# A hybrid decoder layer on one core: reordered dense stage with a 22nd weight slot, and both ends rearranged

## The chip, the core and the metric

The kernel runs on one core of a Trainium2 chip. The metric is the device time of one execution in microseconds, as the median of three runs. TensorE multiplies matrices, VectorE (DVE) and ScalarE (ACT) work on rows of data, GpSimd (POOL) does so too, and SyncE (SP) here issues every transfer from memory. All compute is float32; a "rounded" tile is one in the faster, coarser form that TensorE takes.

## What is computed

One decoder layer over 256 tokens of width 1024, cut to what matters here:

```python
mod = silu(c) @ w_ada + b_ada                       # six vectors: shift, scale, gate, twice
h = rmsnorm(x, norm1) * (1 + sc1) + sh1
proj = h @ w_in                                     # q, k, v | mLSTM q/k, v, o, i/f | gates g_a, g_m
y_a = diff_attention(q, k, v, lam)                  # 4 heads, each the difference of two softmaxes
y_m = rmsnorm(sigmoid(o) * mlstm(silu(conv(qk)), v, i, f))
merged = sigmoid(g_a) * (y_a @ w_br_a) + sigmoid(g_m) * (y_m @ w_br_m)
x = x + gt1 * (merged @ w_out)
h2 = rmsnorm(x, norm2) * (1 + sc2) + sh2
y = sum over 32 experts of gate[e] * ((silu(h2 @ w_e1[e]) * (h2 @ w_e3[e])) @ w_e2[e])   # top 2 of 8 in the top group
out = rmsnorm(x + gt2 * y, norm_f)
```

## The kernel before, in words

All weights pass once from memory, in units of 128 x 2048 floats (1 MB). A **first stage** (to 54 us) multiplies the eight row blocks of q, k and v while VectorE forms the shift and scale that the normalized input needs; each product is done in three passes, rounded weight by rounded input, rounded weight by the input's rest, weight's rest by rounded input.

The **dense stage** (54 to 242 us) works off 24 dense units: `ml0` to `ml3` (mLSTM q and k), `mv`, `mo`, `ga0` to `ga3`, `gm0` to `gm3`, the branch projections (`bra`, `brm`) and the output projection (`wo0` to `wo3`). For each, ACT writes a rounded copy (`split(d)`, line 538, into one of three slots `his`, so it must wait for the job three before), GpSimd subtracts it to leave the rest (line 515, four pieces), and TensorE multiplies (`proj` and `proj_T`, line 1379). Between them stand the attention (`scores` and `sums` on DVE, `exps` and `scale` on ACT, `mix` on DVE, `transpose_a`, `copy_a`, `times_v`) and the mLSTM (gate rows `gate_inputs`, `gate_sums`, `decay`, `numerator`, `hidden`). The 16 conditioning units ("ada") are not multiplied on TensorE: VectorE reduces each against the conditioning vector (`sums_of(i, u)`, line 913, two instructions of 128 x 1024). Dense and ada units come through the same ring of ten slots, in the order of `unit_list`; a slot is loaded again once its last unit was multiplied or summed. SP issues all loads in one fixed order, so a load whose slot is not free holds up all behind it.

The **expert stage** takes the 32 experts in eight quads. A quad needs 12 units (four each of w1, w3 and w2). They land in 21 slots (`XSLOTS`, the ring, the `his` slots and buffers that the dense stage no longer needs); `RELEASES` says which job frees each slot for its first unit, `EARLY` which of these loads are issued among the dense ones. From then on a slot is loaded again when its unit is `used`. A quad gathers its tokens (`gather`), multiplies (`up`, line 1715), transposes the hidden rows (`turn`), multiplies again (`down`, line 1726, in two halves c), VectorE scales each half by the gate (line 1287), and the result is scattered back into four banks that hold the residual sum (`scatter`, line 1670, one part for each c and token tile), while the next quad runs. If a list of tokens is over 32, further passes follow in a branch (`flag`); with these inputs none does.

At the **end** the last scattering waits for `act_end` and `dve_end`, ACT squares the four parts, VectorE makes the norm's factor, and writes each part times factor and gain (line 1335); four stores follow.

Each engine's order is the order of the code; nothing is scheduled. The unit order, the first waits and the place of the sums:

```python
for n, count in enumerate((0, 1, 1, 1, 1, 1, 1, 1, 1, 2, 0, 1, 0, 1, 1, 1, 2, 0, 0, 0)):
    units += [dense[n]] + ada(*sums[:count])
...
for h in range(HEADS):          # VectorE
    conv(h)
    scores(h)
    sums_of(3, h)
```

## Time and profile before

| | us |
|---|---|
| median of three runs | 461.53 (461.12 to 462.02) |
| the profiled execution, its own time | 461.61 |
| its span | 459.8 |
| TensorE busy | 384.4 (84%) |
| VectorE, ScalarE, GpSimd busy | 196.9, 176.5, 154.7 |
| moved from memory | 161.62 MB, 354 GB/s over the span |

A page of the profile lists busy times, then the span in 40 slices, the chain of work that ended last followed back from the end, and the costliest groups of instructions. TensorE has two clocks here, granted by the chip: 1.00 is 2.4 GHz, 0.50 is 1.2 GHz. In a timeline the bracket behind an instruction is the time that its engine had been idle, and what ended it. Busy time alone says little in this kernel, since the stages have different limits; the stretches and timelines show which engine or transfer is waited for in each.

### The profile page before, as it was taken

What the parts mean: (1) busy time and instruction counts of PE and PEld (TensorE: products, weight loads), DVE (VectorE), ACT (ScalarE), POOL (GpSimd) and SP (SyncE); (2) the same over time, 40 slices, a digit from 0 to 9 for tenths busy, and PEclk for the clock granted to TensorE, in tenths of its full rate; (3) what the DMA queues carried; (4) which work ended last, traced back from release to release, by engine and by line L of the source; (5) the groups of instructions that cost most, each with busy time, mean ns of one, the idle gap of its engine ahead of it and who ended that gap; (6) DMA issues with size and microseconds to landing.
All of it is one profiled execution on the core that took longest, in us unless ns stands there. A gap on an engine that the chain in (4) does not pass through costs nothing.

```text
span 459.8 us, 8048 instructions
## 1 busy us (share of the span) xinstructions
PE 384.4 (84%) x3326; PEld 300.4 (65%) x3326; DVE 196.9 (43%) x405; ACT 176.5 (38%) x328; POOL 154.7 (34%) x125
## 2 busy tenths in 40 slices
PE   6699999987799999989989579889897393684963
PEld 5599999887699999989967436445463261351411
DVE  3997369999731538892252130312112003001023
ACT  3677655752937856444253312141212020020012
POOL 0798766658298477869100000000000000000000
PEclk9799999997889999999999989999999799598879
DMA  8999999858849732999996999999999999999932
GB/s 335 423 419 423 419 420 420 295 203 353 324 161 424 240 141 65 386 421 419 406 374 211 427 375 422 424 420 420 420 420 422 422 419 422 420 422 420 422 128 94
DMA packets 23223, 163.23 MB, mean 355 GB/s; under 512 B 2576, under 2 KB 2704, under 8 KB 4368
## 3 DMA queue, kind: packets, MB, share of 16 engines
q1 hardware_dynamic: 23184, 162.68, 87.3%
q8 instruction: 28, 0.46, 0.4%
q14 instruction: 11, 0.09, 0.1%
HBM read 161.62 MB, written 1.05 MB: 354 GB/s over the span
## 4 chain that ended last, share of the span: by engine, by line
PE 58%; DVE 17%; DMA 13%; ACT 5%; issue 3%; SPq 2%; DVEq 0%; ACTq 0%
PE bank L1379 16%; DMA ring<-in_e 12%; PE bank L1715 10%; PE cs_b L1726 6%; PE bank L1681 5%; PE bank L1422 5%; PE bank L1670 4%; DVE ring L913 4%; PE bank L1427 3%; DVE mqk L986 3%; SPq L443 2%; PE cs_b L1379 1%; PE bank L1414 1%; DVE o_att L958 1%; PE cs_b L1408 1%
## 5 line engine op out<-in xcount | busy, mean ns | idle before, releaser
L515 POOL TENSOR_TENSOR ring_r<-ring,his_r 128x512 fp32r<-128x512 f32 x120 | 154.4, 1320 | 54.2 <-ACT his_r L538 54.1
L788 ACT ACTIVATE raw<-bank,sm 128x128 f32<-128x128 f32 x60 | 22.6, 456 | 127.4 <-PE bank L1681 127.4
L1715 PE MATMUL bank<-ring,raw 128*32 128x256 f32 x512 | 55.3, 403 | 9.0 <-DMA ring<-in_e 9.0
L538 ACT ACTIVATE his_r<-ring 128x2048 fp32r<-128x2048 f32 (+1 forms) x32 | 57.6, 1800 | 8.2 <-PE bank L1379 8.2
L1275 DVE TENSOR_TENSOR tmp<-bank,tmp 128x256 f32<-128x256 f32 x8 | 3.4, 425 | 128.0 <-ACT tmp L797 128.0
L1379 PE MATMUL bank<-his_r 128*128 128x256 f32 x304 | 45.2, 293 | 1.9 <-ACT his_r L728 1.2
L1715 PEld LDWEIGHTS bank<-ring,raw 128*32 128x32 f32 x512 | 28.4, 116 | 23.9 <-issue 15.3
L1379 PEld LDWEIGHTS bank<-his_r 128*128 128x128 f32 x304 | 40.4, 197 | 3.7 <-issue 1.4
L913 DVE CUSTOM_DVE_ANT_0 ring<-ring,cs_b 128x1024 f32<-128x1024 f32 x32 | 37.7, 1215 | 0.2
L1681 PEld LDWEIGHTS bank<-const,gm 128*128 128x128 f32 x240 | 28.4, 191 | 9.3 <-issue 7.3
L1681 PE MATMUL bank<-const,gm 128*128 128x128 f32 x240 | 30.1, 278 | 3.4 <-DVE const L1266 1.8
L1670 PE MATMUL bank<-v,const 128*128 128x512 f32 x64 | 29.0, 595 | 1.9 <-DVE sm L1320 1.9
L1715 PE MATMUL bank<-his,raw 128*32 128x256 f32 x176 | 23.3, 390 | 7.9 <-DMA home<-in_e 7.9
L1726 PE MATMUL cs_b<-ring,WT 128*32 128x512 f32 x120 | 26.1, 667 | 2.4 <-DVE WT L1280 1.6
L1379 PE MATMUL bank<-his_r,ring_r 128*128 128x256 f32 x192 | 26.9, 283 | 0.0
L1379 PE MATMUL bank<-hT_r,his_r 128*128 128x256 f32 x192 | 26.6, 280 | 0.0
L1715 PE MATMUL bank<-home,raw 128*32 128x256 f32 x112 | 21.3, 431 | 6.1 <-DMA ring<-in_e 6.1
L1379 PEld LDWEIGHTS bank<-his_r,ring_r 128*128 128x128 f32 x192 | 24.7, 192 | 0.0
L1379 PEld LDWEIGHTS bank<-hT_r,his_r 128*128 128x128 f32 x192 | 24.4, 189 | 0.0
L1287 DVE TENSOR_TENSOR v<-cs_b,o_att 128x512 f32<-128x512 f32 x16 | 11.1, 692 | 28.7 <-PE cs_b L1726 28.7
L1670 PEld LDWEIGHTS bank<-v,const 128*128 128x128 f32 x64 | 11.5, 190 | 15.5 <-issue 15.5
L1379 PE MATMUL bank<-ring_r,his_r 128*128 128x256 f32 x112 | 17.2, 300 | 4.7 <-POOL ring_r L515 4.7
(330 smaller groups left out, 726.2 us busy)
## 6 DMA issues: line engine op xcount, KB each, us to landing
ring<-in_e SPq DMA_DIRECT2D x47, 1024.0 KB, 24.7
ring<-in_rest SPq DMA_DIRECT2D x40, 1024.0 KB, 8.0
his<-in_e SPq DMA_DIRECT2D x16, 1024.0 KB, 22.5
home<-in_e SPq DMA_DIRECT2D x10, 1024.0 KB, 20.5
ring<-in_block SPq DMA_DIRECT2D x8, 768.0 KB, 20.0
o_att<-in_e SPq DMA_DIRECT2D x5, 1024.0 KB, 20.0
mqk<-in_e SPq DMA_DIRECT2D x5, 1024.0 KB, 22.8
qkT<-in_e SPq DMA_DIRECT2D x5, 1024.0 KB, 26.3
```

The lines of the kernel that those rows point to most:

```text
L515: pool.tensor_tensor(ring_r[:, slot_of(n), sl], ring[:, slot_of(n), sl], hi(d)[:, sl].bitcast(F32), ALU.subtract).then_inc(s["w_lo"], 1)
L538: act.activation(hi(d)[:, 0:WIDTH[d]], ring[:, slot_of(n), 0:WIDTH[d]], ACT.Copy).then_inc(s["w_hi"], 1)
L788: ins = act.activation(xg[:, b, k, :], source[:, j * P:(j + 1) * P], ACT.Identity, bias=S("B2", KD)[:, k:k + 1], scale=S("A2", KD)[:, k:k ...
L913: ins = dve.tensor_tensor_reduce(w, w, cs_b[:], 1.0, 0.0, ALU.mult, ALU.add, m2[:, at:at + 1])
L986: ins = dve.scalar_tensor_tensor(out=mqk[:, k, back:T], in0=seq[:, 0:T - back], scalar=col("conv_w", 8 * j + k), in1=mqk[:, k, back:T], op ...
L1379: ins = pe.matmul(out, left(k), right(k), start=(i == 0 and k == 0), stop=(i == 2 and k == nk - 1))
L1422: ins = pe.matmul(pb(f"qk{i // 2}")[:, (i % 2) * T:(i % 2 + 1) * T], w[:, i * P:(i + 1) * P], h, start=start and i % 2 == 0, stop=stop, sk ...
L1427: ins = pe.matmul(pb(f"v{tt}")[:], h[:, tt * P:(tt + 1) * P], w[:, 1024:FIRST], start=start, stop=stop, skip_group_check=True)
L1670: ins = pe.matmul(y_banks[2 * tt + c][:], ptg[:, b, tt, :], outs2[:, 512 * c:512 * c + 512], start=False, stop=stop, skip_group_check=True)
L1681: ins = pe.matmul(target[:, j * P:(j + 1) * P], xn[:, tt, k * P:(k + 1) * P], pone[:, tt].rearrange("p a n -> p (a n)"), start=(tt == 0), ...
L1715: ins = pe.matmul(up_bank[e * CAP:(e + 1) * CAP, half], xg[:, b, k, e * CAP:(e + 1) * CAP], wt[e][:, k, :], start=(k == 0), stop=(k == KD ...
L1726: ins = pe.matmul(out_banks[c][e * CAP:(e + 1) * CAP, :], hidT[:, f, e * CAP:(e + 1) * CAP], wt[e // 2][:, 2 * (e % 2) + f, :], start=(f = ...
```

## The change

In `unit_list` the ada units move behind the fifth dense unit and stand closer together later. On VectorE no sum stands among the four heads: all softmax sums, the gate rows and the mixes come first, then the eight sums of sc2's and sh2's columns in two groups, then the others, all ahead of the attention output's low halves (`y_low`). The gate rows are read from their bank in place of a copy. On ACT each rounded copy goes ahead of the softmax's exponentials or scalings where it stood behind them. The scores of a head are issued as two and two. An unused buffer `free_unit` makes a 22nd expert slot (`SPARE`), for which the mLSTM's weights, the hidden rows, the router's and the i/f weights share other buffers; six expert units in place of three are issued among the dense ones. The first output projection takes its products in a new order, so that it needs only the part of `merged` that is ready. In the last quad the first half is scattered before the second is multiplied; this quad now stands in the else branch of the test on `flag`. The closing squares, factors and outputs are shared anew between ACT and VectorE. `keep_busy` adds eight products after the first squares' sum and three in the last quad, whose results nobody reads.

Three engines around four places. VectorE, between the last head's scores and the value products; before, the last head's last score step (958), two halves of one weight sum (each an ISA pair), the gates' copy and first steps (936 to 940), the first mixes (975) and the next sum:

```order
L958 SCALAR_TENSOR_TENSOR o_att<-bank,const 128x384
L913 ISA ring,sm<-ring,cs_b 128x1024
L913 ISA sm 128x1
L913 ISA ring,sm<-ring,cs_b 128x1024
L913 ISA sm 128x1
L936 COPY o_att<-bank 4x512
L938 TENSOR_SCALAR o_att<-o_att 4x256
L939 TENSOR_TENSOR o_att<-o_att 4x256
...
L969 TENSOR_SCALAR sm<-sm 128x2
L975 SCALAR_TENSOR_TENSOR home<-o_att,sm 128x128
L975 SCALAR_TENSOR_TENSOR home<-o_att,sm 128x256
L913 ISA ring,sm<-ring,cs_b 128x1024
```

and now, where the gate rows are 951 and 952, the mixes 989 and the sums 926:

```order
L972 SCALAR_TENSOR_TENSOR o_att<-bank,const 128x384
...
L951 TENSOR_SCALAR o_att<-bank 4x256
L952 TENSOR_TENSOR o_att<-bank,o_att 4x256
...
L983 TENSOR_SCALAR sm<-sm 128x2
L957 SCALAR_TENSOR_TENSOR o_att<-bank,o_att 4x256
L960 SCALAR_TENSOR_TENSOR o_att<-const,o_att 4x256
...
L989 SCALAR_TENSOR_TENSOR home<-o_att,sm 128x128
L989 SCALAR_TENSOR_TENSOR home<-o_att,sm 128x256
...
L989 SCALAR_TENSOR_TENSOR home<-o_att,sm 128x256
L926 ISA ring,sm<-ring,cs_b 128x1024
L926 ISA sm 128x1
```

The sums went behind all eight mixes, and the copy of the gates' bank is gone.

ScalarE at the same time; before, the gates' exponential and logarithm (616, 618), the scalings of the softmax (594), the value copies (601) and the rounded copies (538):

```order
L538 ACTIVATE his_r<-ring 128x2048
L616 ACTIVATE o_att<-o_att 4x256
L618 ACT_TABLE_LOAD
L618 ACTIVATE o_att<-o_att 4x256
L594 ACTIVATE o_att<-o_att,sm 128x128
L594 ACTIVATE o_att<-o_att,sm 128x256
...
L601 ACTIVATE late<-bank 128x2x2x128
L538 ACTIVATE his_r<-ring 128x2048
L594 ACTIVATE o_att<-o_att,sm 128x128
...
L601 ACTIVATE late<-bank 128x2x2x128
L538 ACTIVATE his_r<-ring 128x2048
```

and now, with the rounded copies at 542, the scalings at 598 and the value copies at 605:

```order
L623 ACTIVATE o_att<-o_att 4x256
...
L625 ACTIVATE o_att<-o_att 4x256
L542 ACTIVATE his_r<-ring 128x2048
L605 ACTIVATE late<-bank 128x2x2x128
L598 ACTIVATE o_att<-o_att,sm 128x128
...
L598 ACTIVATE o_att<-o_att,sm 128x256
L542 ACTIVATE his_r<-ring 128x2048
L605 ACTIVATE late<-bank 128x2x2x128
L598 ACTIVATE o_att<-o_att,sm 128x128
```

The rounded copy that stood ahead of 616 went ahead of the last two heads' exponentials, and the next one stands directly behind the logarithm, ahead of the scalings.

VectorE ahead of the first branch product; before, the mLSTM's last normalized rows (1091), then the low halves of the attention output (1099) and the sums after them:

```order
L1088 RECIPROCAL sm<-sm 128x8
L1091 TENSOR_TENSOR late<-late,sm 128x512 x2
L1099 SCALAR_TENSOR_TENSOR mqk_r<-bank,sm,raw_r 128x512
L1103 MEMSET sm 128x1
...
L913 ISA ring,sm<-ring,cs_b 128x1024
L913 ISA sm 128x1
```

and now, with the rows at 1107 and the low halves at 1118:

```order
L1104 RECIPROCAL sm<-sm 128x8
L1107 TENSOR_TENSOR late<-late,sm 128x512 x2
L926 ISA ring,sm<-ring,cs_b 128x1024
L926 ISA sm 128x1
...
L926 ISA sm 128x1
L932 TENSOR_TENSOR sm<-sm,const 128x8
L1118 SCALAR_TENSOR_TENSOR mqk_r<-bank,sm,raw_r 128x512
L1122 MEMSET sm 128x1
```

Four half sums, or two whole ones, and the closing addition of their columns went between the two.

TensorE at the end; before, the last quad's second products (1726), the jump on `flag` (1775) and the whole scattering (1670):

```order
L1726 MATMUL cs_b<-ring,WT 32x512 x2
L1726 MATMUL cs_b<-his,WT 32x512 x2
L1775 REGISTER_ALU
L1775 COMPARE_AND_BRANCH
L1774 UNCONDITIONAL_BRANCH
L1670 MATMUL bank<-v,const 128x512 x4
```

and now, with the second products at 1782, the scattering at 1726 and the fill-in products at 1383:

```order
L1383 MATMUL bank<-gm,const 128x256 x3
L1747 MATMUL bank<-const,tmp 128x128 x2
L1782 MATMUL cs_b<-ring,tmp 32x512 x8
L1726 MATMUL bank<-v,const 128x512
L1782 MATMUL cs_b<-ring,tmp 32x512 x8
L1726 MATMUL bank<-v,const 128x512 x3
L1855 UNCONDITIONAL_BRANCH
```

One part of the scattering went between the two halves of the second products, the jump ahead of them all.

The diff, cut (buffers that only change their place are left out):

```diff
@@ -64,7 +64,7 @@
...
     sums = [(i, u) for i in (3, 4, 2, 5) for u in range(4)]
-    for n, count in enumerate((0, 1, 1, 1, 1, 1, 1, 1, 1, 2, 0, 1, 0, 1, 1, 1, 2, 0, 0, 0)):
+    for n, count in enumerate((0, 0, 0, 0, 0, 1, 1, 1, 1, 2, 1, 1, 2, 2, 2, 2, 0, 0, 0, 0)):
@@ -89,7 +89,7 @@
...
-XSLOTS = SLOTS + 7
+XSLOTS = SLOTS + 8
@@ -126,13 +126,13 @@
...
-RELEASES = [(X_HOME, "mod"), (ATT, "mixed"), (XN_HOME, "aT3"), (LAST[0], "bra1"),
-            (LAST[1], "sum15"), (LAST[2], "sum16"), (LAST[3], "bra3"), (LAST[4], "brm1"), (MQK, "brm3"), (LAST[5], "brm3")]
+RELEASES = [(SPARE, None), (X_HOME, "mod"), (ATT, "mixed"), (XN_HOME, "aT3"), (LAST[0], "sum15"),
+            (LAST[1], "sum16"), (LAST[2], "bra1"), (LAST[3], "bra3"), (LAST[4], "brm1"), (MQK, "brm3"), (LAST[5], "brm3")]
 RELEASES += [(QKT, "merged"), (LAST[6], "wo0"), (LAST[7], "wo1"), (hi_slot("wo1"), "wo1"), (LAST[8], "wo2"),
              (hi_slot("wo2"), "wo2"), (LAST[9], "wo3"), (hi_slot("wo3"), "wo3"), (SLOTS - 1, "wo3"),
              (HT, "lg"), (LATE, "x2n")]
 ORDER = [i for i, _ in RELEASES]
-EARLY = {NFIRST + 20: (0,), NFIRST + 25: (1,), NFIRST + 27: (2,)}
+EARLY = {NFIRST + 13: (0, 1), NFIRST + 17: (2,), NFIRST + 25: (3,), NFIRST + 36: (4, 5)}
 assert len(set(ORDER)) == XSLOTS
@@ -243,7 +243,8 @@
...
+        free_unit = sb("free_unit", [UNIT])
@@ -607,31 +611,34 @@
...
-            for h in range(HEADS):
+            split(10)
+            tap(0)
+            split(11)
+            for h in range(1, HEADS):
                 tap(h)
-                split(10 + h)
-                exps(h)
-            split(14)
-            act.wait_ge(s["gates"], 2)
+                split(11 + h)
+                exps(h - 1)
+            exps(3)
+            act.wait_ge(s["gates"], 1)
             act.activation(grow[0:4, 2, :], grow[0:4, 2, :], ACT.Exp).then_inc(s["gexp"], 1)
             act.wait_ge(s["gexp"], 1)
             act.activation(grow[0:4, 2, :], grow[0:4, 2, :], ACT.Ln, bias=1.0).then_inc(s["gln"], 1)
+            split(15)
+            values(0)
             scale(0)
             scale(1)
-            values(0)
-            split(15)
             scale(2)
+            split(16)
             values(1)
-            split(16)
             scale(3)
...
+            split(17)
             output_gate(0)
-            split(17)
+            split(18)
             output_gate(1)
-            split(18)
@@ -818,13 +825,19 @@
...
+            for n, (c, tt) in enumerate(((0, 0), (0, 1), (1, 0), (1, 1))):
+                act.wait_ge(s["y_full"], n + 1)
+                act.activation(junk[:, n * 512:(n + 1) * 512], y_banks[2 * tt + c][:], ACT.Square,
+                               accum_out=S("ms5", 4)[:, n:n + 1]).then_inc(s["sq5"], 1)
             for tt in range(TT):
-                for c in range(2):
-                    act.wait_ge(s["y_full"], 2 * tt + c + 1)
-                    act.activation(junk[:, (2 * tt + c) * 512:(2 * tt + c + 1) * 512], y_banks[2 * tt + c][:], ACT.Square,
-                                   accum_out=S("ms5", 4)[:, 2 * tt + c:2 * tt + c + 1]).then_inc(s["sq5"], 1)
                 act.wait_ge(s["var5"], tt + 1)
                 act.activation(S("std5", TT)[:, tt:tt + 1], S("var5", TT)[:, tt:tt + 1], ACT.Sqrt).then_inc(s["std5"], 1)
+            act.wait_ge(s["r5_r"], 1)
+            act.wait_ge(s["y_nf"], 3)
+            for c in (1, 0):
+                sl = slice(512 * c, 512 * c + 512)
+                act.activation(x[:, 0, sl], x[:, 0, sl], ACT.Identity, bias=0.0,
+                               scale=S("r5", TT)[:, 0:1]).then_inc(s["y_out0"], 1)
@@ -930,22 +943,23 @@
...
             def gate_inputs():
...
-                release(dve.tensor_copy(grow[0:4, 0:2, :], pb("ifT")[0:4, :].rearrange("p (a n) -> p a n", a=2)), "ifT")
...
+                dve.tensor_tensor(grow[0:4, 2, :], gate_f, grow[0:4, 3, :], ALU.min).then_inc(s["gates"], 1)
@@ -993,28 +1007,20 @@
...
             for h in range(HEADS):
                 conv(h)
                 scores(h)
-                sums_of(3, h)
-            columns(B2, 3).then_inc(s["mod2"], 1)
             gate_inputs()
             dve.wait_ge(s["lexp"], 1)
             link(dve.tensor_tensor(S("nlam", 1), S("lexp", 2)[:, 1:2], S("lexp", 2)[:, 0:1], ALU.subtract))
             link(dve.tensor_scalar(S("nlam2", 1), S("nlam", 1), -LAMBDA_INIT, None, ALU.add))
-            sums(0)
-            sums(1)
-            mix(0)
+            for h in range(HEADS):
+                sums(h)
+            gate_sums()
+            for h in range(HEADS):
+                mix(h)
+            for u in range(4):
+                sums_of(3, u)
+            columns(B2, 3).then_inc(s["mod2"], 1)
             sums_of(4, 0)
-            sums(2)
...
-            mix(3)
-            sums_of(4, 2)
-            sums_of(4, 3)
@@ -1090,6 +1106,9 @@
...
+            sums_of(5, 2)
+            sums_of(5, 3)
+            columns(S("G2", KD), 5).then_inc(s["gate_c"], 1)
@@ -1111,19 +1130,12 @@
...
-            sums_of(2, 3)
-            sums_of(5, 0)
-            columns(S("G1", KD), 2).then_inc(s["gate_c"], 1)
             gated_a(0)
             gated_a(1)
             y_low("m", 0)
             y_low("m", 1)
@@ -1317,23 +1332,41 @@
...
+            with dve.Else():
+                quad(NQ - 1, NQ - 1, 1, NQ - 1, True, True)
...
+            def gained(n, c, tt):
+
+                sl = slice(512 * c, 512 * c + 512)
+                dve.wait_ge(s["sq5"], n + 1)
+                dve.tensor_tensor(x[:, tt, sl], y_banks[2 * tt + c][:], nfb[:, sl], ALU.mult).then_inc(s["y_nf"], 1)
...
+            gained(0, 0, 0)
+            gained(1, 0, 1)
+            mean_square(0)
+            gained(2, 1, 0)
+            mean_square(1)
...
                 dve.wait_ge(s["std5"], tt + 1)
...
+                own(dve.reciprocal(r5[:, tt:tt + 1], S("std5", TT)[:, tt:tt + 1]), "r5_r", tt + 1)
+            dve.scalar_tensor_tensor(out=x[:, 1, 512:1024], in0=y_banks[3][:], scalar=r5[:, 1:2], in1=nfb[:, 512:1024],
+                                     op0=ALU.mult, op1=ALU.mult).then_inc(s["y_out1"], 1)
+            dve.wait_ge(s["y_nf"], 2)
+            dve.tensor_scalar(x[:, 1, 0:512], x[:, 1, 0:512], r5[:, 1:2], None, ALU.mult).then_inc(s["y_out1"], 1)
@@ -1413,6 +1451,7 @@
...
             filled(ins, "ss")
+            keep_busy(pb("v1")[:, 0:T], squares[:, 0, :], 8)
@@ -1457,10 +1496,10 @@
...
-                for c in range(2):
-                    ps = take(f"s{2 * h + c}")
-                    r = slice(64 * c, 64 * c + 64)
+                two = [(take(f"s{2 * h + c}"), slice(64 * c, 64 * c + 64)) for c in range(2)]
+                for ps, r in two:
                     pe.matmul(ps[:, 0:P], qkT[r, h, 0:P], qkT[r, 4 + h, 0:P], start=True, stop=True)
+                for c, (ps, r) in enumerate(two):
                     filled(pe.matmul(ps[:, P:384], qkT[r, h, P:T], qkT[r, 4 + h, :], start=True, stop=True),
                            f"s{2 * h + c}")
@@ -1602,12 +1641,30 @@
...
-            pe.wait_ge(s["m_hi"], 4)
-            pe.wait_ge(*free("brm3"))
             merged_src = (lambda k: merged_hi[:, k, :], lambda k: merged_lo[:, k, :], (free("brm3"),))
 
             def out_proj(i):
-                proj(f"wo{i}", merged_src, next_dense(8))
+
+                w = next_dense(8)
+                if i:
+                    proj(f"wo{i}", merged_src, w)
+                    return
+                ps = take("wo0")
+                for tt in range(TT):
+                    c = slice(tt * P, (tt + 1) * P)
+                    for ks in ((0, 1, 2, 3, 4, 5), (6, 7)):
+                        if tt == 0:
+                            pe.wait_ge(s["m_hi"], 3 if ks[0] == 0 else 4)
+                        for left, right in ((merged_hi, w[0]), (merged_hi, w[1]), (merged_lo, w[0])):
+                            if tt == 0 and left is merged_lo:
+                                pe.wait_ge(*free(f"brm{ks[-1] // 2}"))
+                            if tt == 0 and right is w[1]:
+                                pe.wait_ge(*w[2][0])
+                            for k in ks:
+                                ins = pe.matmul(ps[:, tt * 256:(tt + 1) * 256], left[:, k, c], right[:, k, :],
+                                                start=(left is merged_hi and right is w[0] and k == 0),
+                                                stop=(left is merged_lo and k == 7))
+                filled(ins, "wo0")
@@ -1754,11 +1810,22 @@
...
+                if final:
+                    keep_busy(token_bank[:, 0:T], xn[:, 0, 0:T], 3)
...
+                if final:
+                    down(r, j, (0,))
+                    pe.wait_ge(s["half_r"], 1)
+                    scatter(b, True, ((0, 0),))
+                    down(r, j, (1,))
+                    scatter(b, True, ((0, 1),))
+                    pe.wait_ge(s["half_r"], 2)
+                    scatter(b, True, ((1, 0), (1, 1)))
+                    return
@@ -1782,9 +1849,11 @@
...
-            pe.wait_ge(s["act_end"], 1)
-            pe.wait_ge(s["dve_end"], 1)
-            scatter(1, True)
+                pe.wait_ge(s["act_end"], 1)
+                pe.wait_ge(s["half_r"], 2)
+                scatter(1, True)
+            with pe.Else():
+                quad((NQ - 1) // LOOP, (NQ - 1) % LOOP, True, True)
```

## Rows read from the trace of the kernel before

**Rows 1.** page, bandwidth (GB/s) of the transfers in 40 equal slices of 11.5 us

```profile
GB/s 335 423 419 423 419 420 420 295 203 353 324 161 424 240 141 65 386 421 419 406 374 211 427 375 422 424 420 420 420 420 422 422 419 422 420 422 420 422 128 94
```

**Rows 2.** chain that ended last, merged: start us, length us, what

```profile
143.62 5.72 PE bank L1379 x48
...
417.55 26.58 DMA ring<-in_e
444.26 3.70 PE cs_b L1726 x16
```

**Rows 3.** stretches: us, busy of PE, PEld, DVE, ACT, POOL, clock, DMA share, GB/s

```profile
247.50:250.00 2.50, 2.50 (x52) 1.45 (x48) 0.00 (x0) 1.94 (x3) 0.00 (x0) 1.00 0.08 29
260.00:420.00 160.00, 123.81 (x1276) 68.66 (x1276) 25.47 (x54) 28.93 (x65) 0.00 (x0) 0.94 1.01 418
```

**Rows 4.** timeline of SyncE: first load into a slot an expert had used

```profile
250.22 0.33 SPq L443 DMA_DIRECT2D home<-in_e  x1
```

**Rows 5.** timeline of TensorE in the dense stage, and three stretches of it

```profile
107.66 2.07 PE L1379 MATMUL bank<-ring_r,his_r 128*128 128x256 f32 x8 [3.14 <-POOL ring_r L515]
...
82.28:129.26 46.98, 38.82 (x272) 36.52 (x271) 43.11 (x80) 29.18 (x44) 28.03 (x23) 0.87 0.80 302
120.00:122.30 2.30, 2.23 (x16) 1.55 (x14) 1.46 (x5) 2.29 (x3) 0.00 (x0) 1.00 0.88 349
142.10:143.40 1.30, 1.30 (x15) 1.30 (x13) 0.00 (x0) 1.08 (x2) 1.30 (x2) 1.00 0.99 416
```

**Rows 6.** timeline of VectorE: a weight sum's half, two mixes, four mixes

```profile
66.50 1.21 DVE L913 CUSTOM_DVE_ANT_0 ring<-ring,cs_b 128x1024 f32<-128x1024 f32 x1
...
103.62 2.86 DVE L975 SCALAR_TENSOR_TENSOR home<-o_att,sm 128x128 f32<-128x128 f32 x2
...
114.82 1.45 DVE L975 SCALAR_TENSOR_TENSOR home<-o_att,sm 128x128 f32<-128x128 f32 x4
```

**Rows 7.** timeline of ScalarE (table load, rounded copy) and of GpSimd (eight rests)

```profile
96.94 1.28 ACT L618 ACT_TABLE_LOAD   x1
100.42 1.90 ACT L538 ACTIVATE his_r<-ring 128x2048 fp32r<-128x2048 f32 x1
...
102.39 10.73 POOL L515 TENSOR_TENSOR ring_r<-ring,his_r 128x512 fp32r<-128x512 f32 x8 [4.79 <-ACT his_r L538]
```

**Rows 8.** timelines of TensorE and VectorE in the first stage

```profile
7.15 4.03 PE L1414 MATMUL bank<-late,const 128*128 128x256 f32 x16
15.92 2.05 PE L1422 MATMUL bank<-his_r 128*128 128x256 f32 x8 [4.75 <-ACT his_r L556]
...
49.63 1.10 PE L1422 MATMUL bank<-hT_r,his_r 128*128 128x256 f32 x8
...
46.66 1.44 DVE L868 TENSOR_TENSOR hT_r<-o_att,his_r 128x256 fp32r<-128x256 f32 x1 [1.84 <-ACT o_att L560]
```

**Rows 9.** page, issues: tile, engine, kind, count, size, median us until landed

```profile
late<-in_x SPq DMA_DIRECT2D x1, 1024.0 KB, 4.7
```

**Rows 10.** timelines of VectorE and TensorE before the first branch product

```profile
176.61 1.54 DVE L1099 SCALAR_TENSOR_TENSOR mqk_r<-bank,sm,raw_r 128x512 fp32r<-128x512 f32 x2 [1.50 <-ACT raw_r L713]
...
180.00 0.64 PE L1379 MATMUL bank<-raw_r,his_r 128*128 128x256 f32 x4
```

**Rows 11.** timeline of TensorE at the first output projection

```profile
206.80 1.19 PE L1379 MATMUL bank<-his_r 128*128 128x256 f32 x8 [1.22 <-ACT his_r L728]
```

**Rows 12.** timeline of TensorE: a head's first score product, and the work after them

```profile
60.13 0.50 PE L1463 MATMUL bank<-qkT 64*128 64x128 f32 x4
...
60.99 0.39 PE L1379 MATMUL bank<-his_r 128*128 128x256 f32 x1
```

**Rows 13.** the end: a stretch, the scattering on TensorE, the last outputs on VectorE

```profile
444.00:446.00 2.00, 1.74 (x12) 0.51 (x16) 0.00 (x0) 0.00 (x0) 0.00 (x0) 0.50 0.03 8
...
449.81 3.67 PE L1670 MATMUL bank<-v,const 128*128 128x512 f32 x8 [1.91 <-DVE sm L1320]
...
455.36 1.41 DVE L1335 SCALAR_TENSOR_TENSOR late<-bank,sm,o_att 128x512 f32<-128x512 f32 x2
```

131 lines of the change are left out of this document (67 added, 64 removed).

## The prediction

> **What bounds the kernel now.** I read the slices of the page first: the transfers run at about 420 GB/s in most of the span, and fall below it between slices 8 and 17 and at the end [rows 1]. The chain of work that ended last then tells where the DMA is the bound: in the second half it is one long run of expert weights, up to the landing at 444.26 us that the last products wait for [rows 2]. The stretches show why it is not the bound everywhere. From 260 to 420 us the DMA is full (1.01, 418 GB/s), but from 247.5 to 250 us it does next to nothing (0.08) [rows 3], and as little in slice 16 [rows 1], while TensorE is busy: every slot is taken, and the queue waits for one to be read. The first expert slot comes free only when the first quad has used it, at 250.22 us [rows 4]. From then on the end is fixed: with 21 slots filled, 75 of the 96 units are left. 1.049 MB at 418 GB/s is 2.51 us, so 75 units take 188 us; they took 444.26 - 250.22 = 194.0 us, with what is lost while the first quads start. So three things set the end: when the compute chain reaches the first quad, how many units are then left, and what comes after the last landing (459.8 - 444.26 = 15.5 us).
>
> The compute chain is TensorE's. Its losses lie between 82.28 and 129.26 us [rows 5]. In these 46.98 us stand five projections of 5.72, 28.6; transposes, columns and the first spread over partitions, 2.3 (the stretch from 120); the second spread, about 0.9; and two value products, 1.3 (what the later two take from 142.1, at full clock): 33.1 us. The other **13.9 us** are idle time (46.98 - 38.82 = 8.2) and a half clock, after the gap of 3.14 us above all. TensorE waits there for rounded weights: ACT makes them in line behind the softmax [rows 7], and the softmax waits for VectorE, where a weight sum of two 1.14 us instructions stands after each head [rows 6].
>
> **The change part by part**, on the profiled execution: span 459.8, its time 461.61, 0.08 over the median of 461.53.
>
> *TensorE kept busy at the start.* The eight added products take 3.9 us at the pace of the sixteen instructions at 7.15 us, and fill most of the idle 4.75 us before 15.92. The first three passes then run at the full clock: about 2.0 us less. But the later blocks wait for the low halves from VectorE: the eighth is ready at 46.66 + 1.44 = 48.1 and is used at 49.63 [rows 8]. VectorE's pace does not hang on the clock, so **1.5** is the most; the least is 0. I take 1.5, since VectorE has hardly a gap there.
>
> *Sums later, rounded copies ahead.* Without 4 x 2.28 us of sums, VectorE is bound by the projections, and ends the fourth head at about 85.4 (they arrive 6.8 us apart, each head takes 5.3). ACT has rounded mo0 by then. The logs of the gates end at 90.1 (two gate rows of 1.3, an exponential and a logarithm of 0.4, a table load of 1.28 [rows 7]), mo1's copy of 1.90 at 92.0, ga0's, behind the value copy and three scalings, at 96.8, all before TensorE wants them (97 and 104). So TensorE runs through to the transposes at 109.4. What is late next: the copy for ga2 stands on ACT ahead of the second output gate and of the copies that the value products need, and its weight sits behind the first sum in SP's queue, for the ring slot is held by the conditioning weights. The mixes: two took 2.86 while GpSimd rounded, four took 1.45 while it did not [rows 6, 7]. Eight mixes at 1.43 from 95 on, and 0.36 once GpSimd pauses at 102, end at 103.4; the sum ends at 105.7, its weight lands 4.7 us later (what the residual's load took, on a queue that was nearly empty [rows 9]), ACT gets through at 114.1, where TensorE could have gone on at 112.5: 1.6 lost. This part gives 13.9 - 1.6 = **12.3**; bounds 9 (the gap is 3 us longer and the clock falls with it) and 13.9.
>
> On this the Trainium skill, SBUF — State Buffer, section "Who interferes with whom", has a rule that speaks against the change: a VectorE instruction with two SBUF inputs and a GpSimd instruction that reads SBUF lock each other out for a whole instruction. The rows agree (1.43 against 0.36 for one mix). By it the gate rows that now read PSUM would escape; the mixes, moved into GpSimd's busy time, would not.
>
> *What is queued behind.* From 105.7 on SP issues without a pause: ga2's weight lands at 110.4 and each next one 2.5 us later, gm0's at 123, gm1's at 130, gm3's at 148, the first branch weight at 155. All but the last are ahead of use. Sums (5,1), (5,2), (5,3) now stand between the last numerator and the low halves of the attention output: 3 x 2.28 = 6.8 us on VectorE. Before, those low halves were ready at 176.61 + 1.54 and TensorE wanted them at 180.00 [rows 10], 1.8 us to spare. The first sum hides behind ACT's squares and the table load (2.1 of 2.28), so 4.7 and the columns come on top: 3.0 us late; with the branch weight late as well, and ACT's squares behind its copy, up to 5. I take **-2.9**; ends -1 and -5.5 (a wait over 3 us also halves the clock).
>
> *Merging.* With no sums on VectorE in the branch products, the merges follow them at once, and the first output projection starts with what is ready: the wait of 1.22 at 206.80 goes [rows 11]. **+1.2**; ends 0 and 1.3.
>
> *Paired scores.* A head takes 60.99 - 60.13 = 0.86 [rows 12]. If both halves ran at once it would be 0.43: at most 1.7 in four heads, at least 0. The eight instructions start 0.11 apart already, near what a 128-column pass takes, so I take **0.2**. The Trainium skill, TensorEngine Tiling (Array Packing), section "Key Properties", says that different row tiles can load and multiply in parallel, and that a change of tiling mode drains the array; by the first the sum would be 1.5 us better, by the second not at all.
>
> The first quad then starts 1.5 + 12.3 - 2.9 + 1.2 + 0.2 = 12.3 us earlier. The DMA follows: from the residual's load on, 20 units are wanted before it, 50 us, and there are some 60.
>
> *The 22nd slot.* 74 units instead of 75 are left at the first release: **2.5**.
>
> *After the last landing.* Before: 3.70 us of products at clock 0.50 (444.26 to 447.96 [rows 2, 13]), then VectorE's scaling and an end mark, scattering from 449.81 for 3.44 (3.67 with the last one's tail), and the last outputs from 455.36. Now the end mark is gone, and one part of the scattering is done before the last landing: products 1.85 at full clock, if three fill-in products hold it, then three parts of 0.86 with the scaling beside the first: 444.26 + 1.85 + 0.05 + 2.58 = 448.74 against 453.25, 4.5 earlier. Squares, root and reciprocal as before; two more small ACT steps in the row cost 0.2, and the outputs are shared by two engines in about the same 1.4. **4.3**; ends 1.0 (clock stays at half, 1.85 more, and the parts slower) and 4.7. The jump on TensorE, now ahead of the last quad, costs nothing, since that quad waits for its weights anyway [rows 2].
>
> Sum: 12.3 + 2.5 + 4.3 = 19.1, so 461.6 - 19.1 = **442.5 us**.
>
> **The rivals.**
> A, the weights come late in the dense stage. SP's queue stops at the first sum; if the mixes and sums end 3 us later than I have them, the value products, the branch wait and the half clock after it take 4 to 5 more: 446.8. For it: the mixes' 1.43; against: slack of 3 to 10 us at most weights. 0.17.
> B, nothing gets in TensorE's way after 130 us: VectorE reaches the low halves in time and the scores overlap, 4.3 better: 438.2. 0.12.
> C, the clock stays low in the tail, as at 444 to 446 us now; the tail gives 1 to 2 only: 445.4. 0.05.
> D, the change does not do what it says, since the transfers alone set the end: then only the slot and the tail count, 454.8. Against it: the idle DMA [rows 3]. 0.03.
> E, slower. The same queue: everything from ga2's weight on waits for the first sum, and from there each us is passed on one to one. It costs more than all gains if that sum ends later than 105.7 + 19.1 = 124.8 us; in the trace the mixes ended at 116.3 with 13.7 us of sums among them. At 127 the time is 463.8. 0.03.
>
> **How the numbers follow.** Forecast 0.60 (its own range 439.5 to 446), A 0.17, B 0.12, C 0.05, D 0.03, E 0.03. The range 438 to 447.5 leaves out D and E, half of B, a third of A, and a little of the forecast's own spread, together 0.2. A measurement here tells 0.2% (0.9 us) from no change: faster 0.96, same 0.01, slower 0.03.
>
> **What would show it.** Start: clock 1.00 from 16 us, the first projection about 1.5 earlier. Dense: no TensorE gap over 1 us from 80 to 110, one of 1 to 2 before the value products, one of 2 to 4 before the first branch product. DMA: busy from 105 to 165, idle for some 8 us before the first quad at 234, 74 units after it. Tail: last products in 1.9 us, 11.2 us from the last landing to the end. Wrong would be: a mix of 0.36 throughout, a long gap at ga2 or at gm0, or half clock in the tail.

## The result, and the profile after

The changed kernel takes 447.8 us (445.5 to 449.7, four runs) against 461.3: a ratio of 0.970, interval 0.966 to 0.975. On record were 442.5 and a range up to 447.5. So the sign was right, and of 19.1 us 13.5 came. Two of the six runs of the changed kernel with no fill-in at the start, below (449.4 and 450.0), lie over 1.5% above its fastest, count as slow and are left out of its row. The profiled execution took 448.08, its span is 446.3 (before 461.61 and 459.8), and all that follows is the difference of these two spans, 13.5.

The transfers on the page (GB/s in 40 slices, now of 11.2 us, against [rows 1]) still pause in slice 16, dip in slice 22 as before (211 in both), and dip lower in slice 24 (289 for 375), in the first quads:

```profile
GB/s 332 422 420 421 419 420 358 291 182 321 421 421 368 377 321 130 398 389 350 333 343 211 423 289 425 423 419 420 419 421 423 420 419 422 420 421 419 420 285 95
```

The timelines of TensorE and, in the last row, SyncE (start, length, engine, line, operands; in the bracket the idle time before it):

```profile
16.62 1.19 PE L1461 MATMUL bank<-his_r 128*128 128x256 f32 x8 [1.30 <-ACT his_r L560]
...
53.78 1.12 PE L1417 MATMUL bank<-his_r 128*128 128x256 f32 x8
...
169.27 0.96 PE L1417 MATMUL bank<-raw_r,his_r 128*128 128x256 f32 x4 [4.35 <-DVE sm L1122]
...
196.10 0.96 PE L1664 MATMUL bank<-his_r 128*128 128x256 f32 x6
...
224.27 1.92 PE L1693 MATMUL bank<-const,hT 128*128 128x36 f32 x8 [0.69 <-ACT hT L760]
226.00 6.18 PE L1708 MATMUL bank<-late,const 128*128 128x512 f32 x8
...
234.07 1.16 PE L1737 MATMUL bank<-const,gm 128*128 128x128 f32 x8
...
241.51 0.33 SPq L445 DMA_DIRECT2D free_unit<-in_e  x1
```

In this order: the first pass of the first stage (before at 15.92 [rows 8]), the first dense projection, the first branch product (before at 180.00 [rows 10]) behind an idle time of 4.35 us that ends with VectorE, the first output projection (before at 206.80 [rows 11]) with no wait, the last logits, the copy of the residual into its banks, the first gather, and the first slot that an expert gives back (before at 250.22 [rows 4]). The stretches beside them (busy TensorE, weight loads, VectorE, ScalarE, GpSimd, clock, DMA share, GB/s):

```profile
82.28:110.43 28.15, 28.15 (x239) 28.15 (x238) 26.29 (x55) 23.20 (x42) 24.18 (x18) 1.00 0.74 287
169.00:173.00 4.00, 3.73 (x18) 3.73 (x19) 0.15 (x2) 0.00 (x0) 3.55 (x3) 0.58 0.51 197
224.00:232.00 8.00, 7.73 (x16) 4.27 (x17) 4.02 (x28) 4.55 (x10) 0.00 (x0) 0.57 0.95 401
246.00:266.00 20.00, 11.80 (x66) 7.22 (x69) 3.75 (x8) 4.67 (x10) 0.00 (x0) 0.74 0.89 363
```

The first is what the reorder was for: the dense products that stood with gaps in [rows 5] run without one at full clock. The other three show a half clock at three places: behind the wait before the branch and at the logits, where the kernel before had the full one (1.00 from 180 to 184 and from 235 to 243 us), and in the first quads, where it had fallen too, but for less long (a mean of 0.91 from 255 to 275 us, against 0.74).

From these rows the sum on record can be drawn up again. "Earlier" is counted from the kernel before; the first release is the sum of the lines above it.

| term | on record | measured | from |
|---|---|---|---|
| first dense projection | 1.5 | 0.5 | 54.32 to 53.78 |
| dense stage up to the last product ahead of the branch | 12.3 + 0.2 | 14.5 | 54.32 to 180.00 before; 53.78 to 164.92 after |
| wait before the first branch product | -2.9 | -4.35 | the bracket at 169.27 (TensorE done at 164.92) |
| half clock behind it, in the branch | in the bounds alone | -1.5 | branch to gates 23.6 before, 25.1 after |
| merging, output projections | 1.2 | 1.5 | gates at 203.64, logits at 235.05 before; 194.40, 224.27 after |
| half clock at the logits and behind | none | -2.0 | 235.05 to 242.78 before, 224.27 to 234.07 after |
| **first release** | **12.3** | **8.7** | 250.22 to 241.51 |
| slot, first quads, up to the last landing | 2.5 | 1.9 | 444.13 to about 433.5 |
| last landing to the end | 4.3 | 2.9 | 15.7 to 12.8 |
| **sum** | **19.1** | **13.5** | 459.8 to 446.3 |

At the logits the last eight products take 0.84 us longer than before and the copy of the residual 2.5 (6.18 for 3.68); a wait of 1.02 us for VectorE, which the kernel before had behind them, is gone in exchange. So 2.0 is the net.

### The profile page after: what moved, and what is told of

Its sections match the earlier page's. It is cut to its first block, busy times and chain, and to the rows that moved or that the text cites. A ratio compares the mean times of both kernels' runs of the same rounds, so it can differ in the third digit from the quotient of the medians.

```text
span 446.3 us, 8095 instructions
## 1 busy us (share of the span) xinstructions
PE 386.6 (87%) x3348; PEld 302.4 (68%) x3348; DVE 190.4 (43%) x403; ACT 177.9 (40%) x330; POOL 156.5 (35%) x125
## 3 DMA queue, kind: packets, MB, share of 16 engines
HBM read 161.62 MB, written 1.05 MB: 364 GB/s over the span
## 4 chain that ended last, share of the span: by engine, by line
PE 71%; DMA 15%; DVE 6%; SPq 3%; ACT 3%; issue 1%; DVEq 0%
PE bank L1417 25%; PE bank L1771 10%; DMA home<-in_e 6%; DMA mqk<-in_e 6%; PE cs_b L1782 5%; PE bank L1737 5%; PE bank L1461 5%; PE bank L1726 4%; SPq L445 3%; PE bank L1466 2%; DMA ring<-in_rest 2%; PE bank L1708 1%; PE cs_b L1417 1%; PE bank L1664 1%; DVE ring L926 1%
## 5 line engine op out<-in xcount | busy, mean ns | idle before, releaser
L519 POOL TENSOR_TENSOR ring_r<-ring,his_r 128x512 fp32r<-128x512 f32 x120 | 156.2, 1336 | 41.0 <-ACT his_r L542 40.9
L1771 PE MATMUL bank<-ring,raw 128*32 128x256 f32 x448 | 44.2, 404 | 7.3 <-DMA mqk<-in_e 7.3
L1417 PE MATMUL bank<-his_r 128*128 128x256 f32 x288 | 41.3, 286 | 0.0
L1417 PEld LDWEIGHTS bank<-his_r 128*128 128x128 f32 x288 | 36.8, 191 | 1.5 <-issue 1.4
L1771 PE MATMUL bank<-his,raw 128*32 128x256 f32 x208 | 25.7, 434 | 11.9 <-DMA late<-in_e 8.1
L1771 PEld LDWEIGHTS bank<-ring,raw 128*32 128x32 f32 x448 | 22.5, 116 | 19.9 <-issue 11.8
L1737 PE MATMUL bank<-const,gm 128*128 128x128 f32 x240 | 31.7, 287 | 3.4 <-DVE const L1278 1.8
L1771 PEld LDWEIGHTS bank<-his,raw 128*32 128x32 f32 x208 | 13.6, 124 | 22.1 <-issue 17.4
L1782 PE MATMUL cs_b<-ring,tmp 128*32 128x512 f32 x128 | 22.2, 629 | 2.1 <-DVE tmp L1292 2.1
L804 ACT ACTIVATE tmp<-bank 128x256 f32<-128x256 f32 x8 | 3.1, 383 | 38.2 <-PE bank L1771 38.2
```

The costliest lines, as they stand in the source:

```text
L519: pool.tensor_tensor(ring_r[:, slot_of(n), sl], ring[:, slot_of(n), sl], hi(d)[:, sl].bitcast(F32), ALU.subtract).then_inc(s["w_lo"], 1)
L1417: ins = pe.matmul(out, left(k), right(k), start=(i == 0 and k == 0), stop=(i == 2 and k == nk - 1))
L1737: ins = pe.matmul(target[:, j * P:(j + 1) * P], xn[:, tt, k * P:(k + 1) * P], pone[:, tt].rearrange("p a n -> p (a n)"), start=(tt == 0), ...
L1771: ins = pe.matmul(up_bank[e * CAP:(e + 1) * CAP, half], xg[:, b, k, e * CAP:(e + 1) * CAP], wt[e][:, k, :], start=(k == 0), stop=(k == KD ...
L1782: ins = pe.matmul(out_banks[c][e * CAP:(e + 1) * CAP, :], hidT[:, f, e * CAP:(e + 1) * CAP], wt[e // 2][:, 2 * (e % 2) + f, :], start=(f = ...
```

## The experiments

Each run's time is set beside the kernel before on the same chip. Spreads of the changed kernel are wide (4 to 5 us, where the kernel before has 2 to 4), so the readings rest on the traces where they can.

| kernel | us, median (range, runs) | ratio, 95% interval |
|---|---|---|
| changed, again | 448.1 (445.5 to 450.4, 6) | 0.974, 0.971 to 0.978 |
| low halves ahead of two sums | 440.4 (438.0 to 443.9, 6) | 0.957, 0.953 to 0.961 |
| changed, 21 slots | 449.9 (448.6 to 451.6, 6) | 0.978, 0.975 to 0.981 |
| changed, no fill-in at the start | 445.6 (441.8 to 446.2, 4 of 6) | 0.967, 0.963 to 0.970 |
| changed, ScalarE's old order | 451.3 (448.6 to 453.4, 4) | 0.979, 0.975 to 0.983 |
| changed, VectorE's old order | 445.3 (443.9 to 449.0, 4) | 0.971, 0.966 to 0.975 |
| low halves first, fill-ins at the waits | 438.1 (437.1 to 439.4, 6) | 0.952, 0.949 to 0.954 |
| low halves first, no fill-in at the start | 440.6 (439.2 to 443.2, 6) | 0.960, 0.956 to 0.963 |
| low halves first, fill-ins, 21 slots | 440.9 (440.3 to 441.4, 5) | 0.958, 0.956 to 0.960 |
| the same with 22 slots, no fill-in in the tail | 438.9 (1) | |
| the same with 22 slots, scattering whole | 440.0 (1) | |
| changed, fill-ins at the waits | 445.6 (444.6 to 446.4, 5) | 0.967, 0.965 to 0.970 |

### The wait before the branch

The term of -2.9 was the first suspect: two sums stand on VectorE ahead of the low halves. VectorE's timeline in the changed kernel (two groups of mixes, then the mLSTM's rows, the first of the four half sums, the addition of the columns, and the low halves):

```profile
93.18 2.04 DVE L989 SCALAR_TENSOR_TENSOR home<-o_att,sm 128x128 f32<-128x128 f32 x6
96.39 2.84 DVE L989 SCALAR_TENSOR_TENSOR home<-o_att,sm 128x128 f32<-128x128 f32 x2 [1.16 <-ACT o_att L598]
...
159.09 2.73 DVE L1107 TENSOR_TENSOR late<-late,sm 128x512 f32<-128x512 f32 x2
161.74 1.21 DVE L926 CUSTOM_DVE_ANT_0 ring<-ring,cs_b 128x1024 f32<-128x1024 f32 x1
...
166.54 1.10 DVE L932 TENSOR_TENSOR sm<-sm,const 128x8 f32<-128x8 f32 x1
167.56 1.53 DVE L1118 SCALAR_TENSOR_TENSOR mqk_r<-bank,sm,raw_r 128x512 fp32r<-128x512 f32 x2
```

The rows end at 161.8, the sums and the columns at 167.6, the low halves at 169.1; TensorE was done at 164.92. The experiment moves the two sums behind the low halves, and nothing else:

```diff
-            sums_of(5, 2)
-            sums_of(5, 3)
-            columns(S("G2", KD), 5).then_inc(s["gate_c"], 1)
 ...
             y_low("a", 0)
             y_low("a", 1)
+            sums_of(5, 2)
+            sums_of(5, 3)
+            columns(S("G2", KD), 5).then_inc(s["gate_c"], 1)
```

> Low halves of the attention output ahead of the sums (5,2) and (5,3) on VectorE, all else as in the changed kernel. Theory 1, these two sums make TensorE wait before the first branch product: the gap of 4.35 us falls under 0.6, the clock stays full behind it, the first output projection starts 5 to 6 us earlier (about 190.5 against 196.1), and the time falls by 4 to 6 us. Rival, the branch weights or ScalarE's squares are just as late: a gap of 2 us or more stays and names them, and less than 3 us is gained. Rival 2, the transfers take over: the first branch product is earlier, but the last landing moves by less than 2 us.

Measured: 440.4, 7.7 less than the changed kernel. The branch product, a stretch behind it, and the first release:

```profile
165.54 0.74 PE L1416 MATMUL bank<-raw_r,his_r 128*128 128x256 f32 x4 [0.79 <-DVE sm L1118]
...
165.00:169.00 4.00, 3.46 (x29) 3.46 (x30) 3.92 (x9) 2.19 (x2) 4.00 (x4) 1.00 0.17 23
...
234.19 0.33 SPq L445 DMA_DIRECT2D free_unit<-in_e  x1
```

The wait is 0.79 and the clock stays at 1.00. The release comes 7.3 us earlier than in the changed kernel, and the span ends 7.5 earlier: in this pair of traces each us in front of the first quad is an us at the end. Theory 1 holds, and neither rival showed. The gain is larger than it said: the branch product starts 3.7 us earlier, the branch takes 23.6 us as in the kernel before (1.5 less than in the changed one), and from the logits to the gather it is 2.1 less, since the clock stayed full there. Whether the last part belongs to the two sums is open (see the clock, below); with fill-in products at the logits in both orders the same two sums still cost over 7 us (445.6 against 438.1). What is left of the wait is no longer VectorE's own: it waits 1.33 us for ScalarE's rounded halves before it starts the low halves at 163.82.

The two sums do have one taker, SyncE: it loads two expert units into their slots, at 164.13 in the changed kernel and at 167.80 here. That stops the transfers for a while (0.17 in the stretch above), and the end shows no cost of it.

### Which part of the dense reorder gives the gain

The change did two things there: sums later on VectorE, rounded copies ahead on ScalarE. Each was undone alone. ScalarE's old order:

```diff
-            split(10)
-            tap(0)
-            split(11)
-            for h in range(1, HEADS):
+            for h in range(HEADS):
                 tap(h)
-                split(11 + h)
-                exps(h - 1)
-            exps(3)
+                split(10 + h)
+                exps(h)
+            split(14)
 ...
```

> The changed kernel with ScalarE's old order between the first projections and the first transposes: rounded copies behind the exponentials and scalings again, the sums stay late on VectorE. Theory 1, the sums on VectorE held up the softmax and with it the copies, so taking them away is nearly all of the gain: TensorE has under 2 us of gaps from 80 to 115 us and the first branch product starts within 2 us of the changed kernel's 169 to 171. Theory 2, the copies ahead matter by themselves: gaps of 4 us or more come back between 95 and 115 us. The wait before the first branch product takes up part of any delay, since there TensorE waits for VectorE: a delay under 4 us in the dense stage costs the end less than 1 us.

```profile
96.00 1.22 PE L1414 MATMUL bank<-ring_r,his_r 128*128 128x256 f32 x8 [1.12 <-POOL ring_r L519]
103.39 1.21 PE L1414 MATMUL bank<-ring_r,his_r 128*128 128x256 f32 x8 [1.41 <-POOL ring_r L519]
...
174.35 1.22 PE L1414 MATMUL bank<-raw_r,his_r 128*128 128x256 f32 x4 [5.02 <-DVE sm L1119]
```

Measured: 451.3, against 448.1, with ranges that overlap, so the times alone do not show that it is slower. TensorE has two gaps of 1.12 and 1.41 between 80 and 115 us (theory 1 said under 2 in all, theory 2 at least 4). It is done ahead of the branch at 169.33, where the changed kernel's traces have 164.9 to 167.2, and goes on at 174.35, where they have 169.3 to 173.4. The delay was not taken up by the wait as I had expected: VectorE's rows, too, end later (166.9 for 161.8), and the wait became 5.02. Both theories missed a part.

VectorE's old order (with the old unit order and early loads, which belong to it):

```diff
             for h in range(HEADS):
                 conv(h)
                 scores(h)
+                sums_of(3, h)
+            columns(B2, 3).then_inc(s["mod2"], 1)
 ...
+            sums(0)
+            sums(1)
+            gate_sums()
+            mix(0)
+            sums_of(4, 0)
 ...
```

> The changed kernel with VectorE's old order (a sum after each head and among the mixes, the low halves ahead of the last sums), the old unit order and the old early loads; ScalarE keeps its rounded copies ahead, and slot, start, first output projection and tail are the changed kernel's. Theory 1, the sums were the cause: gaps of 5 us or more between 80 and 130 us as in the kernel before, the first branch product at 176 to 180, the time 450 to 455. Theory 2, the rounded copies ahead were enough: no gap over 1 us between 80 and 110, the branch product at 165 to 168 without the wait of 4.35, and the time at or under that of the changed kernel.

```profile
101.91 1.22 PE L1419 MATMUL bank<-ring_r,his_r 128*128 128x256 f32 x8 [1.30 <-POOL ring_r L519]
109.87 1.44 PE L1419 MATMUL bank<-his_r,ring_r 128*128 128x256 f32 x8 [2.92 <-POOL ring_r L519]
...
170.56 0.63 PE L1419 MATMUL bank<-raw_r,his_r 128*128 128x256 f32 x4
```

Measured: 445.3, no slower than the changed kernel (the intervals overlap). Each theory has a part: there are gaps (1.30 and 2.92), but few, and the time is not 450 to 455.

The two runs together tell what each half is worth to TensorE, by the time at which it is done ahead of the branch:

| | done at | earlier than before |
|---|---|---|
| before | 180.0 | |
| late sums, old copies | 169.33 | 10.7 |
| copies ahead, old sums | 170.56 | 9.4 |
| both | 164.92 | 15.1 |

Either half alone removes most of the loss, and neither is the larger: the gains overlap, as one would expect where a copy stands in a line behind a softmax and the softmax behind a sum. (The three kernels with a half or both also have the small changes of the start, the scores and the gate rows, which no run took out of the dense stage.) What sets the two runs 6 us apart at the end is the meeting at the branch: with the late sums VectorE comes to the low halves late, and TensorE waits 5.02 us for them; with the old order it does not wait at all. With the low halves first, the late sums do pay: 440.4 against 445.3.

### The clock

Of the three stretches at half clock one stood in the forecast's bounds and two nowhere. First the question whether they belong to the order.

> The changed kernel once more, for its trace. In the trace at hand TensorE's granted clock fell to its lower level at 224 to 232 us and again at 246 to 264 us, where the kernel before kept the full one, and four runs spread over 4 us. If the clock there varies from run to run (theory 1), this trace has it full in at least one of the two places, the first weight release for the experts stands 2 us or more away from 241.5 us, and the times spread by 3 us or more again. If the drops belong to the new order (theory 2), they stand at the same two places and the release is at 241.5 within 0.5 us.

Measured: 448.1 (445.5 to 450.4). The clock fell again behind the wait at the branch, at 226 to 232 us and at 260 to 263, but also at 113 to 116, where TensorE had no gap over 0.3 us in front; the release stood at 243.0, 1.5 later, and the end 1.2 earlier. A row of TensorE and two stretches of that trace (columns as above):

```profile
110.66 1.97 PE L1545 MATMUL bank<-o_att,const 4*128 4x256 f32 x8
...
104.00:113.00 9.00, 9.00 (x71) 8.31 (x70) 8.90 (x16) 3.76 (x5) 9.00 (x8) 1.00 1.01 424
113.00:117.00 4.00, 4.00 (x23) 4.00 (x22) 3.97 (x14) 1.91 (x1) 1.21 (x2) 0.58 1.01 426
```

TensorE is busy through both, and the second is at 0.58. So neither theory holds as it stands: the places behind waits recur, and some falls come without one. The fall at 113 us recurs too, in seven of the thirteen traces of kernels with the change or a part of it, each time within 1 us of the end of the products with four rows (110.66 above).

Over all traces without fill-ins at the place:

| wait of TensorE | us | the clock fell |
|---|---|---|
| before the first branch product, sums first | 4.35 to 6.22 | 6 of 6 |
| in the first quad, before the second products | 4.30 | 9 of 9 |
| before the first quad's next gather | 1.79 | 3 of 9 |
| before the second gather | 1.59 to 1.60 | 0 of 9 |
| at the logits, for ScalarE | 0.69 | 6 of 9 |
| before the first branch product, low halves first | 0.21 to 0.97 | 0 of 4 |

At the logits it fell for 3 to 7 us, and not in the kernel before, with the low halves first, and with VectorE's old order. Five of these six traces are of kernels that had waited over 4 us at the branch, some 55 us before; the sixth (low halves first, no fill-in at the start) had not. The fall in the gather can be read at the end of the kernel: from the first release to the end it is 204.6 to 204.8 us in the three traces that have it, and 202.0 to 203.3 in the other traces of kernels with 22 slots and the tail's pieces.

A fill-in product ahead of that wait, and three, three and eight at the waits of the first quad, test the price (each product is two instructions in the trace):

```diff
             turn_x(3)
+            keep_busy(pb("rank")[:, 0:T], hT[:, 0, :], 1)
             pe.wait_ge(*free("x2T3"))
 ...
+                if first:
+                    keep_busy(out_banks[0][:, 0:T], xn[:, 0, 0:T], 3)
                 if not last:
                     pe.wait_ge(s["pg_ready"], it + 2)
                     gather(0)
+                if first:
+                    keep_busy(out_banks[0][:, 0:T], xn[:, 0, 0:T], 3)
 ...
+                if first:
+                    keep_busy(out_banks[0][:, 0:T], xn[:, 0, 0:T], 8)
```

> As the kernel with the low halves first (440.4 us), with fill-in products at TensorE's waits: one ahead of the last logits (a wait of 0.69), three, three and eight in the first quad's waits (1.79, 1.59 and 4.30), results read by nobody. Theory, the clock's falls in the first quad cost 2 to 3 us there and hold the release of slots back: with the fills the clock stays at 1.00 from 238 to 258 us, the first gather takes 2.05 in place of 3.65, the first second-half products 3.64 in place of 5.6, and the time falls by 1 to 3 us. Rival, the queue has enough filled slots to bridge it (75 MB are still to come): the time stays within 1 us. Rival 2, the clock falls all the same.

The last logits, the two gathers and the stretch of the first quad:

```profile
220.43 1.08 PE L1692 MATMUL bank<-const,hT 128*128 128x36 f32 x8 [0.25 <-ACT hT L760]
242.01 2.05 PE L1737 MATMUL bank<-const,gm 128*128 128x128 f32 x16 [0.40 <-DVE const L1277]
245.65 2.05 PE L1737 MATMUL bank<-const,gm 128*128 128x128 f32 x16 [0.30 <-ACT raw L795]
...
238.00:256.00 18.00, 15.19 (x114) 11.36 (x110) 3.49 (x9) 4.67 (x10) 0.00 (x0) 1.00 1.01 422
```

Measured: 438.1, 2.4 less, with intervals that just touch, and six runs within 2.3 us where they had 5.9. The waits have shrunk from 0.69, 1.79 and 1.59 to 0.25, 0.40 and 0.30, both gathers take 2.05, and the clock is 1.00 in the whole quad. This kernel is the fastest of all here, 9.7 us under the changed one.

The same fill-ins on the changed kernel itself:

> The changed kernel with the fill-in products at the last logits and in the first quad, sums where the changed kernel has them. Theory, of the 5.6 us that the forecast was short some 2 are the low clock at 224 to 232 us (products on the path that took 3.7 in place of 6.2) and up to 2 that in the first quad: 445 to 446, and a spread under 3 us. Rival, the clock falls there because of the wait of 4 to 6 us at the first branch product, and falls with the fills too: 447 to 448.

```profile
171.07 1.22 PE L1417 MATMUL bank<-raw_r,his_r 128*128 128x256 f32 x4 [5.30 <-DVE sm L1122]
226.19 1.08 PE L1693 MATMUL bank<-const,hT 128*128 128x36 f32 x8 [0.25 <-ACT hT L760]
```

Measured: 445.6, as the theory said, and a spread of 1.8, against 448.1 and 5.0: some 2.5 of the missing 5.6 us are the clock at the logits and in the first quad. The wait before the branch is still there (5.30), with its fall, and the clock did not fall at the logits in spite of it. It fell there in none of the five traces with the fill-in. What the fill-ins do is not taken apart: they shorten the wait, and they put products of 256 columns behind the narrow ones (36 columns at the logits, four rows at 110 us) that stand in front of several of the falls. Whether the wait or the narrow work matters, no run separates.

The Trainium skill, TensorE: Matmul & The Clock Gate, section "Why this matters for your kernels", advises against idle gaps between bursts of matmuls; the traces agree, since each of the fifteen waits of 4.30 us or more in the table came with a fall, and are stricter, since one of 0.69 us was in six of nine. No run here shows what the chip looks at.

### The start

> Without the eight fill-in products at the start. The forecast said that they give 1.5 us, and the first dense projection came 0.54 earlier. Theory 1, the full clock of the first three passes is worth 2 us but the sum of squares ends 0.7 later and the first low half is waited for: the projection starts at 54.3, 0.5 later than with the products, clock 0.50 from 16 to 21 us, and the sum of squares ends at 11.2. Theory 2, the products delay the start by themselves: without them the sum of squares ends at 11.9 all the same.

```diff
             filled(ins, "ss")
-            keep_busy(pb("v1")[:, 0:T], squares[:, 0, :], 8)
```

Measured: the clock is at 0.50 from 15 to 21 us, the sum of squares ends at 11.3, and the first dense projection starts at 54.48. That is theory 1. Yet the later end of that sum in the changed kernel's first trace (11.9) is not shown to be the products' doing: with them it ends anywhere from 10.8 to 12.1.

The same edit with the low halves first:

> As the kernel with the low halves first (440.4 us), without the eight fill-in products at the start. By the traces the products let the first dense projection start 0.5 to 0.9 us earlier, yet the changed kernel without them had a lower median (446.0 against 448.1, spreads of 4 to 8 us). Theory 1, the start is worth its 0.5 and the medians were chance: 440.9 plus or minus 1. Theory 2, a longer unbroken stretch of products brings more falls of the clock later: without the fills the time is 438 to 439 and the mean granted clock of the runs higher.

The first pass and the first dense projection with the low halves first and no fill-in at the start:

```profile
15.91 2.04 PE L1459 MATMUL bank<-his_r 128*128 128x256 f32 x8 [4.96 <-ACT his_r L560]
...
54.06 1.12 PE L1416 MATMUL bank<-his_r 128*128 128x256 f32 x8
```

The first pass takes 2.04 for its eight in place of 1.19, and the projection starts at 54.06 against 53.62 with the products, 0.4 us. Over all traces it is more: eleven with the products start it at 53.0 to 54.0 (median 53.3), the three without at 54.06, 54.32 and 54.48, so they are worth some 1.0 us there. In the timed runs it is lost in the spread: 440.6 against 440.4. On the changed kernel the run without them seems lower, but its six times (441.8 to 450.0, mean 446.4) overlap widely with the six with them (445.5 to 450.4, mean 448.1), and with the low halves first nothing of it is left. That the products cost something later is not shown.

### The slot

```diff
-XSLOTS = SLOTS + 8
+XSLOTS = SLOTS + 7
-RELEASES = [(SPARE, None), (X_HOME, "mod"), ...
+RELEASES = [(X_HOME, "mod"), ...
 ...
-EARLY = {NFIRST + 13: (0, 1), NFIRST + 17: (2,), NFIRST + 25: (3,), NFIRST + 36: (4, 5)}
+EARLY = {NFIRST + 13: (0,), NFIRST + 17: (1,), NFIRST + 25: (2,), NFIRST + 36: (3, 4)}
```

> The unused buffer is no expert slot: 21 slots again, five expert loads among the dense ones in place of six. What it leaves out is one load ahead of the first release. Theory, 2.51 us for the unit left over: slower than the changed kernel by 2.5 us, with 75 units behind the first release. Rival, the queue has slack at the first quads (it stood 2.5 us idle at 262 to 265 us in the changed kernel): slower by less than 1 us.

> As the kernel with the low halves first and the fill-in products (438.1 us, six runs within 2.3 us), with 21 slots. On the changed kernel the slot came out at 1.8 us (449.9 against 448.1), under spreads of 3 to 5 us. Theory 1, a slot is one unit of 2.51 us off the end: 440.6. Theory 2, part of it is given back, since a queue that fills its last slot sooner also stands idle sooner before the first release: 439 to 440.

Measured: 1.8 us on the changed kernel, inside its spread, and 440.9 against 438.1 on the quieter one, 2.8 us with ranges that do not touch. The slot is worth its unit of 2.51, within what can be told: theory 1.

### The tail

In the changed kernel the chain that ended last no longer goes through the last landing (start, length, what):

```profile
396.17 27.97 DMA home<-in_e
...
424.28 3.66 PE bank L1771 x64
...
430.37 1.99 PE cs_b L1782 x16
...
432.38 0.70 DVE v L1299
...
433.13 1.13 PE bank L1726 x2
434.26 1.85 PE cs_b L1782 x16
436.11 1.98 PE bank L1726 x4
...
440.57 0.75 DVE late L1366
```

It comes from the last weight of the first products (424.14). The second half's weights had landed by about 433.5 (stretches of 1 us, and at the end those of the four stores):

```profile
433.00:434.00 1.00, 0.87 (x2) 0.30 (x2) 0.08 (x1) 0.00 (x0) 0.00 (x0) 1.00 0.10 41
434.00:435.00 1.00, 1.00 (x9) 0.29 (x12) 0.00 (x0) 0.69 (x2) 0.00 (x0) 1.00 0.00 0
442.00:443.00 1.00, 0.00 (x0) 0.00 (x0) 0.00 (x0) 0.00 (x0) 0.00 (x0) 0.84 1.04 387
443.00:444.00 1.00, 0.00 (x0) 0.00 (x0) 0.00 (x0) 0.00 (x0) 0.00 (x0) 0.50 1.03 379
444.00:445.00 1.00, 0.00 (x0) 0.00 (x0) 0.00 (x0) 0.00 (x0) 0.00 (x0) 0.50 0.54 195
```

but this half starts at 434.26, since the first half's scaling and scattering stand in front.

> As that kernel without the three fill-in products in the last quad. Theory 1, they hold TensorE's clock over the waits of the tail: without them the last quad's second products run at 0.50 (3.7 us for each 16 in place of 1.9) and the stretch from the last landing to the end is 14 to 16 us in place of 12.1. Theory 2, the clock stands at 1.00 anyway after the 3.7 us of first products (415.7 to 419.4), and the tail stays at 12.1 within 0.3.

```diff
                 if final:
-                    keep_busy(token_bank[:, 0:T], xn[:, 0, 0:T], 3)
```

Measured: the second products at 592 ns each, at full clock, and the end at 437.1, 202.4 behind its first release; with the fill-ins 202.0. Theory 2: in this one run the clock stood without them. So the full clock of the tail, which I had put down to the fill-ins, can come without them.

> As that kernel, with the last quad's second products in one piece and all four parts of the scattering behind them. Theory 1, the part that now stands between the halves saves its 0.9 to 1.1 us at the end, less the time that it holds the second half up (that half starts 0.2 to 0.8 after its weights have landed): without it the second half starts at the landing, and the end comes 0.3 to 0.8 us later. Theory 2, the part costs as much as it saves: the same within 0.2.

```diff
-                    down(r, j, (0,))
-                    pe.wait_ge(s["half_r"], 1)
-                    scatter(b, True, ((0, 0),))
-                    down(r, j, (1,))
-                    scatter(b, True, ((0, 1),))
-                    pe.wait_ge(s["half_r"], 2)
-                    scatter(b, True, ((1, 0), (1, 1)))
+                    down(r, j)
+                    pe.wait_ge(s["half_r"], 2)
+                    scatter(b, True, ((0, 0), (0, 1), (1, 0), (1, 1)))
```

```profile
397.63 26.67 DMA ring<-in_e
...
424.44 1.98 PE cs_b L1782 x16
...
426.44 0.70 DVE v L1298
...
427.19 2.86 PE bank L1726 x6
```

Measured: the second half starts at its landing, but all four parts of the scattering then follow the scaling, and the end lies 13.8 us behind the last landing and 203.6 behind the first release. With the pieces it was 202.0 behind the release, and some 12.6 behind a last landing at about 425. By these the piecewise order is worth 1.2 to 1.6 us, more than the 0.3 to 0.8 expected: it also hides VectorE's scaling (0.70) behind a part. This is one run of each, and with the same tail the distance from release to end was 202.0 in one trace and 202.8 in another.

## Why the prediction was off

**Right.** What bounds the kernel: the transfers at the end, the compute chain up to the first release. With the low halves first the release moved by 7.3 and the end by 7.5. The copies for mo1 and ga0 were in time, as worked out, and no gap over 0.3 us stood from 80 to 110. Merging gave 1.5 for 1.2, the slot its 2.5. VectorE was to have the low halves ready at 168.9, and TensorE went on at 169.27. Part of that is luck: a dense stage that gave 2.0 more made up for a start that gave 1.0 less, and both ran into the same wait.

**The mixes** were sized too high: I took 1.43 us for each of eight while GpSimd works. Six took 2.04 together, 0.34 each, and only the last two 1.42 each, though GpSimd has a record through all of it. The first sum ended at 101.4 in place of 105.7, ga2's copy was early enough, and the 1.6 us expected ahead of the value products did not come. The prediction had weighed the rule of the Trainium skill, SBUF — State Buffer, section "Who interferes with whom", by which each of these mixes contends with a GpSimd instruction that reads SBUF. Two of eight agree with it (1.42); six do not, the measurement decides, and why they escaped is open. Rival A rested on this and did not happen.

**The step that failed is the price of the waits: TensorE's clock behind them.** The sum has TensorE at full clock from the branch to the end. Behind the wait before the first branch product the half clock cost 1.5 us; it stood in the bounds (-5.5) and belonged into the value. At the logits it cost 2.0 and was no term at all, and in the first quads most of the 0.6 that the slot's line is short; the fill-ins at these two places gave back 2.5. Together that is up to 4.1 of the missing 5.6 us. I had read the falls of the kernel before as tied to gaps of over 1 us, and took the full clock for granted where no gap was added. The wait of 0.69 at the logits was there before, without a fall. Rival C placed this risk in the tail alone, where it did not occur.

**The wait itself** was mis-sized with it. Its end was placed within 0.4 us, but I priced it from TensorE at 166.0, and TensorE was there at 164.92: most of what the dense stage gained beyond the forecast, the wait took back. Wait and clock together took 5.8 where 2.9 stood on record. "B, nothing in the way after 130" had 0.12 for 4.3 us; the experiment that clears the way gave 7.7. I had looked at the three sums as something that comes late anyway and hides, and did not ask what their order buys: they end at 167.6, and TensorE takes nothing from them before 194.40.

**Which half of the reorder works.** The prediction put the dense stage's loss down to one chain, copies behind the softmax behind the sums. That holds, and it means that cutting it at either place would have given most of the gain (10.7 or 9.4 of 15.1 us). The prediction did not say so.

**The start** gave 0.5, not 1.5: the sum of squares ended 0.7 later in this trace and the first low half was waited for 0.44 us; the other traces with these products have the projection at 53.0 to 54.0, so 1.0 is their usual gain. **Paired scores** gave nothing: 0.85 for 0.86 a head. **The tail**: 4.3 forecast and 2.9 measured. The last products wait 0.8 us for the first half's part of the scattering and not for their weights, and the four stores now start together: at the 380 to 390 GB/s of the rows at 442 and 443 us their 1.05 MB takes 2.7 us, so 4.6 us pass from VectorE's last output to the end, where it was 3.0.

## What to carry to other kernels

When a stage is sped up, ask of each queue which steps in front of the next meeting point nobody waits for yet, and move those behind it: two sums in the wrong place kept 7.7 us from a change that gave 13.5. Undo each half of a reorder alone before believing which one works, and read both runs at the same point: here either half alone brought TensorE 9 to 11 us forward, both brought 15, and at the end of the kernel the moved sums showed nothing until the low halves were put first. A wait on TensorE costs its length and then, often but not each time, some us of half clock; fill-in products into a free bank, placed in the wait, took away 2.5 us and some 60% of the spread.

## What the runs showed of the hardware

The clock fell within about 1 us of a wait of only 0.69 us in six traces of nine, and at 113 to 118 us in seven with no wait over 0.3 us in the 10 us in front, each time just behind products with four rows. The Trainium skill's advice above is about idle gaps, and these seven falls have none in front. Four stores of 256 KB issued within 2 us filled the queue (share 1.04 and 1.03, 387 and 379 GB/s), so here the end of the kernel was not the last output but the last megabyte, and about an us more. And the last loads do not land at the end of the full rate: the DMA's share went 0.74, 0.49, 0.29, 0.10 over the last four us in the changed kernel, and the kernel before waited 1.05 us for such a straggler.
